# A decoder layer on one core: earlier ScalarE tables, query roots by logarithm and exponential, and a shorter TensorE program ahead of the head-pair loop

## The chip, the cores and the metric

The kernel runs on one core of one Trainium2 chip, in one launch. The metric is device time in microseconds. Three runs of the kernel before gave a median of 1426.36 us. All times below are microseconds from the start of the profiled span, unless ns is written.

## The reference

One decoder layer over x of 1024 tokens by 1024 channels, with 256 memory tokens. All of it is float32.

```
hn = rms_norm(x, attn_norm)
q, k, v, xq = split(hn @ sb_w_in, [1024, 1024, 1024, 256])
# stick-breaking attention, 16 heads of 64, causal
z = q k^T / 8
a = sigmoid(z) * product of sigmoid(-z) over the later keys before the query
mix = a v
# cross attention, 4 heads of 64, into the memory
mk, mv = split(rms_norm(mem, mem_norm) @ w_mem_kv, [256, 256])
p = softmax(rms_norm(xq per head, xq_norm) (rms_norm(mk per head, xk_norm))^T / 8)
cross = p mv
x = x + concat(mix, cross) @ w_out
x = x + (silu(h @ w_gate) * (h @ w_up)) @ w_down,   h = rms_norm(x, ffn_norm)
```

rms_norm(y, g) is y / sqrt(mean(y*y) + 1e-6) * g.

## The kernel before, in words

Every engine has its own program, with the order of its work written out by hand; semaphores join them. Operands of the large products are split in a high and a low part (names ending in _h and _l), and each product is three matmuls: high by high, high by low, low by high. ScalarE writes the high part (a Copy with rounding), VectorE the low part (a subtraction).

**Start.** SyncE loads x in 8 tiles of 128 tokens. For each tile `act_root` takes the sum of squares (Square with an accumulated sum) and the root of the mean (Sqrt), and `dve_scale` inverts the root and scales the tile. TensorE first runs WARM matmuls of the identity by the identity (128 columns, float32, result unused), then transposes x (L716). The first transposes wait until tiles 0 to 3 are scaled. The identity is made by GpSimd, which then fills `fail` with ones (L1561); `s_id` counts these constants.

**Memory and queries of the cross attention.** The queries of its four heads come in two groups of two heads, called `x_` 0 and 1. Those of group 1 are projected in the four pieces `pe_project_in(pe, MW, 0..3)` (L284, 12 matmuls of 512 columns each). The sum of squares of each query head is a matmul of the squared queries by `half_ones` (two columns): `pe_cross_stat(pe, x_)`, eight matmuls L843 in a row, for group 0 after piece 0 and for group 1 in turn 0 of the cross loop. Each float32 matmul stands in the records as two matmuls and two weight loads. `act_cross_stat` takes the root with Sqrt, `dve_cross_stat` inverts it and makes the scales `q_stat` for the softmax.

**Cross loop.** Sixteen turns c, written out without a loop instruction. In each, TensorE makes the scores of turn c+2 (L877), transposes the weights of turn c (L915), in every second turn sums the values (L944), and runs up to 12 matmuls L284 that project q, k and v for head pair 0 (`pe_piece`). ScalarE copies the transposed weights (`act_cross_high`) and takes Exp for turn c+2 (L897). The value sums and the sums of squares of both groups share one PSUM bank, `o_ps`. Then the first head pair is opened: scores L341, Sigmoid on ScalarE (L422, L428).

**Pair loop.** `pe_step` handles one head pair and projects the next pair's q, k, v (L313); it transposes the weights (L351), sums values (L367), and closes with the eight transposes of v (L324). Six of the steps are in a loop instruction with two steps in its body, run three times (376 matmuls a step). The output projection and the FFN follow; the FFN too has a loop instruction, run four times.

Of the kernel before, what the change touches and what calls it, by code (L numbers as in the profile page):

```python
# [19 lines left out]
def trunk(nc, x, mem, norms, w_mem_kv, w_out, w_gate, w_up, w_down, sb_w_in, out):  # L20
# [35 lines left out]
    with ExitStack() as ctx:  # L56
# [212 lines left out]
        def pe_project_in(pe, n, piece, out=j_ps, only=None, left=None):  # L269

            wh, wl = w_h[n // 2 % 2], w_l[n // 2 % 2]
            hf, q = (piece % 4) // 2, piece % 2
            if q == 0 and only != 1:
                pe.wait_ge(s_wl, n + hf + 1)
            for c in (2 * q, 2 * q + 1) if only is None else (2 * q + only,):
                kc = 4 * hf + c
                parts = [(i, half) for i in range(3) for half in range(2)]
                if kc == 0:
                    parts.sort(key=lambda p: p[1])
                for i, half in parts:  # L280
                    if kc == 0 and i == 0 and left:
                        left(half)
                    w, h = ((wh, hh), (wh, hl), (wl, hh))[i]
                    mm = pe.matmul(out[:, half], w[:, hf, c], h[:, kc, half * BANK:(half + 1) * BANK],  # L284
                                   start=(kc == 0 and i == 0), stop=(kc == KC - 1 and i == 2))
            if q == 1 and only != 0:
                mm.then_inc(s_pj, 1)

        def pe_piece(pe, s, piece, first=False, only=None):
            b = piece // 4  # L290

            def left(half):
                if first and b == 0:
                    pe.wait_ge(s_sq, 1 + half)
                else:
                    pe.wait_ge(s_eh, 6 * s + 2 * b - 1 + half)
                    if b:
                        pe.wait_ge(s_el, 4 * s + 2 * b - 1 + half)
            pe_project_in(pe, W0 + 6 * s + 2 * b, piece, only=only, left=left)
# [304 lines left out]
        s_ql = sem("cross_q_low_done")  # L604
        s_ct = sem("cross_weights_transposed")
# [73 lines left out]
        WARM = 12  # L679
# [156 lines left out]
        def pe_cross_stat(pe, x_):  # L836

            pe.wait_ge(s_sq, 2 * x_ + 2)
            if x_:
                pe.wait_ge(s_qr, 1)  # L840
            for c in range(x_ * NT, x_ * NT + NT):
                t = c % NT
                mm = pe.matmul(o_ps[:, 2 * c:2 * c + 2], xq_sq[:, x_, t * P:(t + 1) * P], half_ones[:, :],  # L843
                               start=True, stop=True)
            mm.then_inc(s_qs, 1)

        def act_cross_stat(act, x_):
            n = slice(2 * NT * x_, 2 * NT * (x_ + 1))
            act.wait_ge(s_qs, x_ + 1)
            act.activation(q_stat[:, 0, n], o_ps[:, n], ACT.Sqrt, bias=eps_col[:, :], scale=1.0 / HD).then_inc(s_qr, 1)  # L850

        def dve_cross_stat(dve, x_):
            n = slice(2 * NT * x_, 2 * NT * (x_ + 1))
            dve.wait_ge(s_qr, x_ + 1)
            dve.reciprocal(q_stat[:, 1, n], q_stat[:, 0, n]).then_inc(s_qi, 1)
            dve.wait_ge(s_qi, 3 * x_ + 1)
            dve.tensor_scalar(q_stat[:, 2, n], q_stat[:, 1, n], CQ, None, ALU.mult).then_inc(s_qi, 1)
            dve.tensor_scalar(q_stat[:, 3, n], q_stat[:, 1, n], -CQ, None, ALU.mult).then_inc(s_qi, 1)
            dve.wait_ge(s_qi, 3 * x_ + 3)
# [50 lines left out]
        def pe_cross_turn(pe, c):  # L910
            pe.wait_ge(s_cp, 2 * c + 2)
            if c >= 2:
                pe.wait_ge(s_ctl, c - 1)
            for b in range(4):
                mm = pe.transpose(t_ps[:, c % 2, b * P:(b + 1) * P], csucc[:, c % GR, b * P:(b + 1) * P], ident[:, :])  # L915
            mm.then_inc(s_ct, 1)
# [685 lines left out]
        def _(act):  # L1602
            act.wait_ge(s_id, 1)
            for t in range(4):
# [38 lines left out]
            for c in range(CU):  # L1643
                act_cross_high(act, c)
                if c == 0:
                    act_cross_stat(act, 1)
                if c + 2 < CU:
                    act_cross_exp(act, c + 2)
                if c in X_EVAC:
# [5 lines left out]
                if c in X_CONV:  # L1655
                    act_w(act, X_CONV[c] // 6, X_CONV[c] % 6, X_CONV[c] // 6)
            act.wait_ge(s_pj, W0 + 6)
# [59 lines left out]
        def _(dve):  # L1717
# [48 lines left out]
            for c in range(CU):  # L1766
# [8 lines left out]
                if c == 0:  # L1775
# [72 lines left out]
        def _(pe):  # L1848
            pe.wait_ge(s_id, 3)

            for _ in range(WARM):
                pe.matmul(ps[:, 3, 0:P], ident[:, :], ident[:, :], start=True, stop=True)
# [21 lines left out]
            pe_project_in(pe, MW, 0, xq_ps[1])  # L1874
            pe.wait_ge(s_id, MADE)
            pe.wait_ge(s_mka, MT + 2)
            pe.wait_ge(s_mv, MT)
            pe_cross_stat(pe, 0)
# [7 lines left out]
            pe_project_in(pe, MW, 2, xq_ps[1])  # L1886
            pe.wait_ge(s_xl, XU0)
# [5 lines left out]
            for c in range(CU):  # L1893
                if c + 2 < CU:
                    pe_cross_scores(pe, c + 2)
                if c == 0:
                    pe_cross_stat(pe, 1)
# [3 lines left out]
                for k in range(X_FIRST + sum(X_COUNT[:c]), X_FIRST + sum(X_COUNT[:c + 1])):  # L1901
                    pe_piece(pe, 0, k // 2, first=True, only=k % 2)
            pe_scores(pe, 0, 0, 0, first=True)
# [47 lines left out]
```

## Time and profile before

| what | value |
|---|---|
| median of 3 runs | 1426.36 us (1424.12 to 1427.22) |
| the profiled execution | 1431.33 us |
| its span | 1429.5 us |
| PE busy in the span | 96% |
| ACT busy, DVE busy | 46%, 66% |
| mean granted clock of PE | 0.981 |
| chain of work that ended last, by engine | PE 90%, ACT 4%, DVE 2%, issue 2% |

The profiled execution took 1.83 us beyond its span, and 4.97 us more than the median of the runs. PE is TensorE's matmuls, PEld its weight loads, ACT ScalarE, DVE VectorE, POOL GpSimd, SPq the queue of SyncE that issues transfers. A time in square brackets at the end of a line of the timeline is the idle time of the engine before it, with what ended it.

### The profile page before, as it was taken

To read this page: it belongs to the slowest core of one execution; us is meant where nothing else is said; L and a number is where in the kernel's file an instruction comes from. 1 tells how busy PE (TensorE), PEld (TensorE's weight loads), DVE (VectorE), ACT (ScalarE), POOL (GpSimd) and SP (SyncE) were. 2 spreads that over 40 slices of the span, in tenths; PEclk is the share of its full clock that TensorE was granted. 3 is DMA by queue.
4 is the path that set the end of the run, shared out by engine and by line. 5 is a ranking of instruction groups with operands and counts; after the bars stand their busy time and mean duration, and the time that the engine had idled before them with its cause. 6 is when DMAs were issued, how large, how long until landed. Compare 5 with 4: busy or idle time off the path is not lost.

```text
span 1429.5 us, 20494 instructions
## 1 busy us (share of the span) xinstructions
PE 1377.2 (96%) x6988; PEld 1127.6 (79%) x6988; DVE 949.7 (66%) x1346; ACT 655.3 (46%) x1120; POOL 186.3 (13%) x155
## 2 busy tenths in 40 slices
PE   6999999899989999699999999999999999999999
PEld 5777788788878888577887788888888888888887
DVE  5567879687968888786347857455565645656455
ACT  7566566566666666573245413324232232422321
POOL 0000000000000000214014311112111120211200
PEclk9989999999999999899999999999999999999999
DMA  6100101001000101003300212111112111121103
GB/s 236 30 17 22 30 23 31 24 23 30 23 23 23 37 17 44 30 23 110 104 16 15 89 52 66 45 47 43 63 42 64 51 44 59 44 60 58 44 30 133
DMA packets 90136, 70.23 MB, mean 49 GB/s; under 512 B 3792, under 2 KB 75472, under 8 KB 90064
## 3 DMA queue, kind: packets, MB, share of 16 engines
q1 hardware_dynamic: 90064, 69.23, 15.6%
q8 instruction: 50, 0.82, 0.3%
q14 instruction: 22, 0.18, 0.0%
HBM read 65.03 MB, written 4.19 MB: 48 GB/s over the span
## 4 chain that ended last, share of the span: by engine, by line
PE 90%; ACT 4%; DVE 2%; issue 2%; POOL 1%; DMA 1%; SPq 0%; ACTq 0%; DVEq 0%; POOLq 0%
PE ps L1284 27%; PE ps L313 17%; PE ps L1380 17%; PE ps L987 7%; PE ps L367 5%; PE ps L351 5%; PE ps L341 4%; PE ps L284 3%; PE ps L1064 1%; ACT junk L687 1%; PE ps L776 1%; POOL f L1144 1%; PE ps L716 1%; PE ps L915 1%; PE ps L877 1%
## 5 line engine op out<-in xcount | busy, mean ns | idle before, releaser
L1390 DVE TENSOR_TENSOR x<-ps,x 128x512 f32<-128x512 f32 x176 | 121.6, 691 | 71.2 <-PE ps L1380 67.0
L436 ACT ACTIVATE a_h<-ps 128x256 fp32r<-128x256 f32 (+2 forms) x96 | 78.0, 812 | 145.6 <-PE ps L351 145.6
L1296 ACT ACTIVATE kept<-ps 128x512 f32<-128x512 f32 x60 | 35.7, 595 | 236.0 <-PE ps L1284 236.0
L313 PE MATMUL ps<-hh,w_h 128*128 128x512 f32 x336 | 142.0, 423 | 0.0
L1380 PE MATMUL ps<-dw_h,gu_l 128*128 128x512 f32 x352 | 138.5, 394 | 0.0
L1380 PE MATMUL ps<-dw_l,gu_h 128*128 128x512 f32 x352 | 137.5, 391 | 0.0
L1380 PE MATMUL ps<-dw_h,gu_h 128*128 128x512 f32 x352 | 137.0, 389 | 0.3 <-issue 0.3
L313 PE MATMUL ps<-hh,w_l 128*128 128x512 f32 x336 | 133.5, 397 | 0.0
L313 PE MATMUL ps<-hl,w_h 128*128 128x512 f32 x336 | 133.1, 396 | 0.0
L545 DVE TENSOR_TENSOR a_l<-ps,a_h 128x256 fp32r<-128x256 f32 (+2 forms) x96 | 91.5, 953 | 60.5 <-ACT a_h L436 59.9
L1284 PE MATMUL ps<-ft_h,part_l 128*128 128x512 f32 x320 | 126.5, 395 | 0.0
L1284 PE MATMUL ps<-ft_l,part_h 128*128 128x512 f32 x320 | 125.2, 391 | 0.0
L1284 PE MATMUL ps<-ft_h,part_h 128*128 128x512 f32 x320 | 124.5, 389 | 0.0
L519 DVE TENSOR_TENSOR_SCAN fail<-fail,own 128x129 f32<-128x129 f32 (+3 forms) x128 | 107.7, 869 | 1.3 <-ACT fail L422 1.3
L1254 DVE TENSOR_TENSOR part_l<-part_x,part_h 128x512 fp32r<-128x512 f32 x140 | 94.3, 691 | 5.3 <-ACT part_h L1247 2.8
L351 PE MATMUL ps<-ident,succ 128*128 128x128 f32 x576 | 82.0, 279 | 13.6 <-DVE a_l L545 8.6
L1284 PE MATMUL ps<-f_h,part_l 128*128 128x512 f32 x240 | 94.7, 395 | 0.0
L1284 PE MATMUL ps<-f_h,part_h 128*128 128x512 f32 x240 | 93.5, 389 | 0.6 <-DVE part_l L1254 0.6
L1284 PE MATMUL ps<-f_l,part_h 128*128 128x512 f32 x240 | 93.8, 391 | 0.0
L532 DVE TENSOR_TENSOR succ<-fail,succ 128x256 f32<-128x256 f32 (+2 forms) x96 | 93.6, 975 | 0.3
L1308 DVE TENSOR_TENSOR kept<-ps,kept 128x512 f32<-128x512 f32 x30 | 20.7, 691 | 104.0 <-PE ps L1284 104.0
L552 POOL TENSOR_TENSOR o_t<-o_t,pv_low 128x256 f32 x24 | 23.7, 986 | 497.8 <-ACT o_t L448 497.8
(217 smaller groups left out, 3141.9 us busy)
## 6 DMA issues: line engine op xcount, KB each, us to landing
w_raw<-in_sb_w_in SPq DMA_DIRECT2D x52, 256.0 KB, 2.9
dw_x<-in_w_down SPq DMA_DIRECT2D x22, 512.0 KB, 3.3
part_x<-in_w_gate SPq DMA_DIRECT2D x40, 256.0 KB, 3.5
part_x<-in_w_up SPq DMA_DIRECT2D x40, 256.0 KB, 2.9
wo_raw<-in_w_out SPq DMA_DIRECT2D x20, 256.0 KB, 2.8
x_in<-in_x SPq DMA_DIRECT2D x8, 512.0 KB, 7.8
x<-in_x SPq DMA_DIRECT2D x16, 256.0 KB, 5.7
out<-x SPq DMA_DIRECT2D x16, 256.0 KB, 2.0
```

Source lines behind the costliest of these rows:

```text
L313: mm = pe.matmul(j_ps[:, 0], w[:, kc // 4, kc % 4], h[:, kc, half * BANK:(half + 1) * BANK], start=(kc == 0 and i == 0), stop=(kc == KC - ...
L351: mm = pe.transpose(t_ps[:, h, j * P:(j + 1) * P], succ[:, u % 2, h, j * P:(j + 1) * P], ident[:, :])
L367: mm = pe.matmul(o_ps[:, h * 2 * P + q0:(h + 1) * 2 * P], v_s[par][:, k0 // P + j, 2 * h:2 * h + 2, :].rearrange("p a d -> p (a d)"), a[:, ...
L436: act.activation(a_h[:, :, 0:w // P, col * P:(col + 1) * P], t_ps[:, :, 0:w].rearrange("p h (j q) -> p h j q", q=P), ACT.Copy).then_inc(s_ ...
L519: dve.tensor_tensor_scan(back, back, own[:, BANK - w:BANK + 1][:, ::-1], 0.0, ALU.mult, ALU.max).then_inc(s_scan, 1)
L532: done = dve.tensor_tensor(g, f[:, :, 1:w + 1], g, ALU.mult)
L545: dve.tensor_tensor(a_l[:, :, 0:w // P, c], t_ps[:, :, 0:w].rearrange("p h (j q) -> p h j q", q=P), a_h[:, :, 0:w // P, c].bitcast(F32), A ...
L987: mm = pe.matmul(out_bank(i), o[k][:, t * P:(t + 1) * P], w[:, k], start=(at_ == 0 and j == 0), stop=(at_ == len(order) - 1 and j == 2))
L1254: dve.tensor_tensor(part_l[m][p][:, :, :].rearrange(flat), part_x[m][p][:, :, :].rearrange(flat), part_h[p][:, :, :].rearrange(flat).bitca ...
L1284: mm = pe.matmul(product_bank(m, p), w[:, k], g[:, k], start=(p in (0, 1, 3) and k == 0 and i == 0), stop=(k == 3 and i == 2), skip_group_ ...
L1380: mm = pe.matmul(ps[:, (2, 3, 0, 1)[d % 4]], g[:, fb, t * P:(t + 1) * P], w[n][:, fb], start=(fb == 0 and i == 0), stop=(fb == FB - 1 and ...
L1390: dve.tensor_tensor(o, ps[:, (2, 3, 0, 1)[d % 4]], o, ALU.add).then_inc(s_x2, 1)
```

## The change

- ScalarE gets two activations whose results nobody reads: a Sqrt of one column before it waits for the first tile of x, and a Sigmoid of one column in turn 13 of the cross loop.
- The root and its reciprocal for the queries are taken as exp(-0.5 ln(mean + eps)): Ln, then Exp on ScalarE, in place of Sqrt on ScalarE and a reciprocal on VectorE.
- The eight small matmuls of group 0 are placed one by one behind the first eight large matmuls of piece 0, and write to the bank of the scores, `z_ps[:, 1]`, in place of `o_ps`. Those of group 1 move from turn 0 to turn 1 of the cross loop, four behind each of its two half pieces. ScalarE's part for group 1 moves behind Exp of turn 3, VectorE's part to turn 2.
- The first matmuls are 5 of 512 columns (identity by `fail`, float32) in place of 12 of 128 columns, and wait for the fourth constant in place of the third.
- TensorE no longer waits for `s_ctl` before the transposes of turns 2 to 15.

```
-        def pe_project_in(pe, n, piece, out=j_ps, only=None, left=None):
+        def pe_project_in(pe, n, piece, out=j_ps, only=None, left=None, stat=None):
...
+                    if stat is not None and stat % NT < 6 * (c % 2) + 2 * i + half + 1 <= NT:
+                        pe_cross_stat(pe, stat // NT * NT + 6 * (c % 2) + 2 * i + half)
...
-        WARM = 12
+        WARM = 5
...
-        def pe_cross_stat(pe, x_):
-
-            pe.wait_ge(s_sq, 2 * x_ + 2)
-            if x_:
-                pe.wait_ge(s_qr, 1)
-            for c in range(x_ * NT, x_ * NT + NT):
-                t = c % NT
-                mm = pe.matmul(o_ps[:, 2 * c:2 * c + 2], xq_sq[:, x_, t * P:(t + 1) * P], half_ones[:, :],
-                               start=True, stop=True)
-            mm.then_inc(s_qs, 1)
+        def cross_stat_ps(x_):
+            return (z_ps[:, 1], o_ps)[x_]
+
+        def pe_cross_stat(pe, c):
+
+            x_, t = c // NT, c % NT
+            if t == 0:
+                pe.wait_ge(s_sq, 2 * x_ + 2)
+            mm = pe.matmul(cross_stat_ps(x_)[:, 2 * t:2 * t + 2], xq_sq[:, x_, t * P:(t + 1) * P], half_ones[:, :],
+                           start=True, stop=True)
+            if t == NT - 1:
+                mm.then_inc(s_qs, 1)
 
         def act_cross_stat(act, x_):
             n = slice(2 * NT * x_, 2 * NT * (x_ + 1))
             act.wait_ge(s_qs, x_ + 1)
-            act.activation(q_stat[:, 0, n], o_ps[:, n], ACT.Sqrt, bias=eps_col[:, :], scale=1.0 / HD).then_inc(s_qr, 1)
+            act.activation(q_stat[:, 0, n], cross_stat_ps(x_)[:, 0:2 * NT], ACT.Ln, bias=eps_col[:, :], scale=1.0 / HD
+                           ).then_inc(s_ql2, 1)
+            act.wait_ge(s_ql2, x_ + 1)
+            act.activation(q_stat[:, 1, n], q_stat[:, 0, n], ACT.Exp, scale=-0.5).then_inc(s_qr, 1)
 
         def dve_cross_stat(dve, x_):
             n = slice(2 * NT * x_, 2 * NT * (x_ + 1))
             dve.wait_ge(s_qr, x_ + 1)
-            dve.reciprocal(q_stat[:, 1, n], q_stat[:, 0, n]).then_inc(s_qi, 1)
-            dve.wait_ge(s_qi, 3 * x_ + 1)
...
         def pe_cross_turn(pe, c):
             pe.wait_ge(s_cp, 2 * c + 2)
-            if c >= 2:
-                pe.wait_ge(s_ctl, c - 1)
...
             act.wait_ge(s_id, 1)
+            act.activation(rms[:, 0:1], eps_col[:, :], ACT.Sqrt)
...
             for c in range(CU):
                 act_cross_high(act, c)
-                if c == 0:
-                    act_cross_stat(act, 1)
                 if c + 2 < CU:
                     act_cross_exp(act, c + 2)
+                if c == 1:
+                    act_cross_stat(act, 1)
...
+                if c == CU - 3:
+                    act.activation(x_stat[:, 0, 0:1], eps_col[:, :], ACT.Sigmoid)
...
-                if c == 0:
+                if c == 2:
                     dve_cross_stat(dve, 1)
...
-            pe.wait_ge(s_id, 3)
-
+            pe.wait_ge(s_id, 4)
             for _ in range(WARM):
-                pe.matmul(ps[:, 3, 0:P], ident[:, :], ident[:, :], start=True, stop=True)
+                pe.matmul(ps[:, 3], ident[:, :], fail[:, 0, 0, 0:BANK], start=True, stop=True)
...
-            pe_project_in(pe, MW, 0, xq_ps[1])
             pe.wait_ge(s_id, MADE)
-            pe.wait_ge(s_mka, MT + 2)
-            pe.wait_ge(s_mv, MT)
-            pe_cross_stat(pe, 0)
+            pe_project_in(pe, MW, 0, xq_ps[1], stat=0)
             pe_project_in(pe, MW, 1, xq_ps[1])
...
             pe_project_in(pe, MW, 2, xq_ps[1])
+            pe.wait_ge(s_mv, MT)
+            pe.wait_ge(s_qr, 1)
             pe.wait_ge(s_xl, XU0)
             pe_cross_scores(pe, 0)
...
                 if c == 0:
-                    pe_cross_stat(pe, 1)
+                    pe.wait_ge(s_sq, 2 * XP)
                 pe_cross_turn(pe, c)
                 if c % 2 == 0 and c:
                     pe_cross_values(pe, c // 2 - 1)
-                for k in range(X_FIRST + sum(X_COUNT[:c]), X_FIRST + sum(X_COUNT[:c + 1])):
+                k0 = X_FIRST + sum(X_COUNT[:c])
+                for k in range(k0, k0 + X_COUNT[c]):
                     pe_piece(pe, 0, k // 2, first=True, only=k % 2)
+                    if c == 1:
+                        for t in range(4 * (k - k0), 4 * (k - k0) + 4):
+                            pe_cross_stat(pe, NT + t)
```

## Rows read from the trace of the kernel before

**Rows 1.** The page: busy time, share of the span, instructions, by engine.

```profile
PE 1377.2 (96%) x6988; PEld 1127.6 (79%) x6988; DVE 949.7 (66%) x1346; ACT 655.3 (46%) x1120; POOL 186.3 (13%) x155
```

**Rows 2.** Windows: stretch, its length, busy time (instructions) by engine, granted clock.

```profile
57.60:61.00 3.40, 3.40 (x10) 2.60 (x9) 0.78 (x3) 0.03 (x1) 0.00 (x0) 0.50 0.27 77
74.60:84.90 10.30, 8.99 (x27) 6.59 (x26) 4.00 (x12) 6.96 (x14) 0.00 (x0) 0.50 0.09 27
142.90:146.40 3.50, 3.50 (x11) 2.58 (x9) 2.55 (x4) 0.00 (x0) 0.00 (x0) 0.51 0.00 0
264.00:391.50 127.50, 122.85 (x756) 101.86 (x755) 103.13 (x127) 81.10 (x131) 7.90 (x8) 0.99 0.09 26
854.30:975.50 121.20, 121.20 (x530) 99.13 (x529) 69.66 (x101) 35.85 (x61) 20.72 (x17) 1.00 0.18 53
```

**Rows 3.** Timeline of the start, all engines: start, length, instruction.

```profile
1.47 1.82 POOL L1561 MEMSET fail<- 128x2064 f32 x1
...
1.58 5.22 PE L1852 MATMUL ps<-ident 128*128 128x128 f32 x24 [1.58 <-POOL ident L1559]
...
4.20 1.28 ACT L687 ACT_TABLE_LOAD   x1 [4.20 <-DMA x_in<-in_x]
...
6.66 1.28 ACT L689 ACT_TABLE_LOAD   x1
...
10.89 1.04 ACT L687 ACTIVATE junk<-x_in 128x1024 f32<-128x1024 f32 x1
...
13.39 3.52 PE L716 MATMUL ps<-ident,x_in 128*128 128x128 f32 x16 [6.59 <-DVE x_in L696]
```

**Rows 4.** DMA issues of 2.62 to 2.65: size, us from issue to landing.

```profile
x_in<-in_x SPq DMA_DIRECT2D x1, 512.0 KB, 7.3
```

**Rows 5.** Timeline of the cross attention and the loop's opening, all engines.

```profile
54.88 1.92 PE L843 MATMUL ps<-half_ones,xq_sq 128*128 128x2 f32 x16 [0.26 <-DVE mv L1749]
...
61.09 0.60 PE L1883 MATMUL ps<-ident,mk_raw 128*128 128x128 f32 x4
...
71.47 0.38 PE L877 MATMUL ps<-mk_h,q_h 64*128 64x256 f32 x2
...
76.85 1.28 ACT L897 ACT_TABLE_LOAD   x1
...
78.85 0.58 PE L877 MATMUL ps<-mk_h,q_h 64*128 64x256 f32 x1 [1.31 <-ACT succ L897]
...
85.51 0.39 PE L877 MATMUL ps<-mk_h,q_h 64*128 64x256 f32 x2
...
...
86.47 0.36 PE L944 MATMUL ps<-a_h,mv 128*128 128x256 f32 x1
...
140.28 0.44 PE L341 MATMUL ps<-k_h,q_h 64*128 64x384 f32 x2 [1.41 <-ACT succ L428]
```

**Rows 6.** Timeline of PE in the pair loop: one place of each step, and the jumps.

```profile
210.38 0.66 PE L351 MATMUL ps<-ident,succ 128*128 128x128 f32 x4 [1.01 <-DVE a_l L545]
...
268.86 0.44 PE L341 MATMUL ps<-k_h,q_h 64*128 64x384 f32 x2 [2.62 <-issue]
276.10 0.66 PE L351 MATMUL ps<-ident,succ 128*128 128x128 f32 x4 [1.02 <-DVE a_l L545]
337.61 0.66 PE L351 MATMUL ps<-ident,succ 128*128 128x128 f32 x4 [1.01 <-DVE a_l L545]
...
396.74 0.69 PE L341 MATMUL ps<-k_h,q_h 64*128 64x384 f32 x2 [3.19 <-issue]
...
404.96 0.66 PE L351 MATMUL ps<-ident,succ 128*128 128x128 f32 x4 [1.02 <-DVE a_l L545]
```

**Rows 7.** Transfers of program code, 264.2 to 265.4: packets, MB.

```profile
q8 instruction: 2, 0.03, 17.7%
```

**Rows 8.** The same, 265.4 to 392.4.

```profile
q8 instruction: 7, 0.11, 0.4%
```

**Rows 9.** The same, 854 to 1339, the whole run of the FFN loop.

```profile
q8 instruction: 5, 0.08, 0.1%
```

More of the change, by code:

```diff
@@ L285, in pe_project_in, with pe_piece @@
                                    start=(kc == 0 and i == 0), stop=(kc == KC - 1 and i == 2))
+                    if stat is not None and stat % NT < 6 * (c % 2) + 2 * i + half + 1 <= NT:
+                        pe_cross_stat(pe, stat // NT * NT + 6 * (c % 2) + 2 * i + half)
             if q == 1 and only != 0:
                 mm.then_inc(s_pj, 1)
-        def pe_piece(pe, s, piece, first=False, only=None):
+        def pe_piece(pe, s, piece, first=False, only=None, stat=None):
             b = piece // 4
@@ L298, in left @@
                         pe.wait_ge(s_el, 4 * s + 2 * b - 1 + half)
-            pe_project_in(pe, W0 + 6 * s + 2 * b, piece, only=only, left=left)
+            pe_project_in(pe, W0 + 6 * s + 2 * b, piece, only=only, left=left, stat=stat)
         def pe_part(pe, s, par, p, lo):
@@ L604, in trunk @@
         s_ql = sem("cross_q_low_done")
+        s_ql2 = sem("cross_q_logs_taken")
         s_ct = sem("cross_weights_transposed")
@@ L854, in dve_cross_stat @@
             dve.wait_ge(s_qr, x_ + 1)
-            dve.reciprocal(q_stat[:, 1, n], q_stat[:, 0, n]).then_inc(s_qi, 1)
-            dve.wait_ge(s_qi, 3 * x_ + 1)
             dve.tensor_scalar(q_stat[:, 2, n], q_stat[:, 1, n], CQ, None, ALU.mult).then_inc(s_qi, 1)
             dve.tensor_scalar(q_stat[:, 3, n], q_stat[:, 1, n], -CQ, None, ALU.mult).then_inc(s_qi, 1)
-            dve.wait_ge(s_qi, 3 * x_ + 3)
+            dve.wait_ge(s_qi, 2 * x_ + 2)
         def dve_cross_q(dve, b):
```

## The prediction

> **What bounds the kernel.** I read the page first: TensorE is busy for 1377.2 us of the span of 1429.5 [rows 1], and it carries 90% of the chain of waits, so only what lets TensorE start earlier, wait less or run at a higher clock counts. Then the granted clock by windows, which shows stretches at half clock (1.2 GHz, the other level being 2.4). Three of them lie in the part that the change touches: 57.6 to 61.0, 74.6 to 84.9, 142.9 to 146.4 [rows 2]. A matmul of 512 columns costs 0.23 us at full clock (121.2 us for 530 [rows 2]), so a stretch at half clock loses half of the time that TensorE is busy in it. Last I read the timeline ahead of each stretch, to see what TensorE did before its clock fell, and the program code transfers around the jumps of the two loops.
>
> **1. The start: 1.1 us.** ScalarE loads a table when x arrives, at 4.20, and another for Sqrt at 6.66 [rows 3]. The new Sqrt moves one load ahead of the wait and makes the other needless: Square runs under Sqrt's table too (10.89, no load before it [rows 3]). That is twice 1.28 us off ScalarE, but x doesn't come so early. Tile 3 is issued at 2.62 and takes 7.3 us [rows 4]: it lands at 9.95 or so, and its Square can begin at 10.05 in place of 10.89. So 0.84 us, and the first transposes start at 12.55 in place of 13.39. They ran before at half clock (16 in 3.52 us against 0.60 us for 4 at 61.09 [rows 3, 5]). TensorE had ended its first matmuls at 6.8, and waited 6.59 us. The new ones have 4 times the columns for 5/12 of the count: 1.67 x 5.22 = 8.7 us at the rate of [rows 3], less if the clock rises on the way, from 3.3 (the fill of `fail` ends then [rows 3]). They end between 9 and 12.0, before 12.55. If the clock then stands at full, the first copy by ScalarE starts 0.3 to 0.6 us earlier. I take 0.84 + 0.3 = 1.1, bounds 0.5 and 1.5. From there the same chain of roots leads on, and tile 4 (behind the four) isn't late by more than it was.
>
> **2. Sums of squares, group 0: 1.7 us.** From 54.88 to 61.09 TensorE does 16 small matmuls in 1.8 us and 12 large ones. At full clock that is 1.8 + 12 x 0.23 = 4.6 us; it took 6.2, and 0.26 of idle stood before it [rows 5]. The clock fell right behind the small ones. Spread between large matmuls, no stretch holds small ones alone for more than 0.25 us, so I take it that the clock stays: 1.6 + 0.26, less 0.2 for weight loads that the mixing bares. Bounds: 0.1 if the clock falls all the same, 1.9. ScalarE's Ln and Exp, with loads, lie in its wait for the transposes at 61.09.
>
> **3. Group 1: 3.9 us.** From 71.47 to 85.51 TensorE spends 14.0 us [rows 5]. What is in it at full clock: two sets of scores and two of transposes (0.96 us a turn, from 85.51 to 86.47 [rows 5]) 1.9, small matmuls 1.8, 18 large ones 4.2; sum 7.9. The other 6.1 are half clock over 9.0 busy us [rows 2] and the wait of 1.31 for Exp, which stood behind Sqrt and two loads (the second at 76.85 [rows 5]). The price of the new order: the value sums of turn 2 share a bank with the small sums, and wait until ScalarE's Exp for group 1 is done. The traces place a load by the next function alone: a set without Sqrt at 4.20, then another [rows 3]. So I expect Ln to load a set of its own, and Exp to load the old one again: 2 x 1.28 + 2 x 0.3 = 3.2 us from the last small matmul, of which TensorE covers 0.96 with scores and transposes. It waits 2.2 us; queued behind are six large matmuls and the scores of turn 5, and ScalarE's Exp for turn 4 waits too, which nobody needs before those. 6.1 - 2.2 = 3.9. Bounds: 2.2 (the clock falls in that wait, 1.7 us as at 57.6) and 6.1 (no load between Ln and Exp, no wait).
>
> The Trainium skill ("ScalarE: Activation LUTs", Table sets: the hidden batching unit) says that ln and then exp cost one load, since one set holds both. No row here shows Ln. By that rule, if the set is the one chosen, a load is spared and the wait of this step shrinks to about 0.9 us or nothing: 5.2 to 6.1 in place of 3.9.
>
> **4. The loop's opening: 2.8 us.** The load for Sigmoid stood between the last copies of the cross loop and the first Sigmoid; TensorE waited 1.41 us for it at 140.28 [rows 5]. In turn 13 ScalarE has waits that hold a load. That gives 1.3. With 1.3 of 2.5 us idle gone, the half clock from 142.9 to 146.4 [rows 2] likely goes too: 1.7 us more. I take 1.3 + 1.5; bounds 1.3 and 3.0. If the cover were gone, the load would delay the copies of turn 14 by 1.28 us.
>
> **5. The jumps of the pair loop: 9.9 us.** A step takes 61.51 us (276.10 to 337.61), but 65.72 (210.38 to 276.10) and 67.35 (337.61 to 404.96) where the loop jumps back [rows 6]: 4.2 and 5.8 dearer, made of idle 2.62 and 3.19 with nobody to wait for, and of a lower clock behind it. Program code comes in pieces of 16 KB. At the jump two are fetched within 1.2 us [rows 7], 7 more in the rest of the pass [rows 8], the last of them (392.4) just ahead of the next jump. So from one jump to the next there are 9 pieces, the first being the loop's head, which is fetched again each time: it had been dropped. The FFN loop is jumped three times with no fetch at all: 5 pieces in its first pass, none later [rows 9]. Its body has 530 matmuls against 752 [rows 2], or 6 pieces touched and one fetched ahead: 7 are kept, 9 aren't. The last piece of the pair loop is entered just before the jump: 1.1 us lies at most between the two fetches of [rows 7], in which TensorE does 8 or 9 matmuls with their loads, some 20 instructions. The change takes away 7 float32 matmuls of two matmuls and two loads, and 14 waits: 42 instructions ahead of the loop. The loop then ends in the piece before, and its passes need 8. If 8 are kept, both jumps cost nothing: 10.0 less 0.1. Below, nothing is saved if they aren't.
>
> The Trainium skill ("Runtime: NRT & Kernel Launch", Instruction fetch mechanics) gives TensorE room for 2048 instructions in blocks of 16 KiB; an estimate from it is 8 blocks, so the loop would just fit. The same section says that a jump outside a window of two pages forces a fetch. By that the jumps go on costing 10.0 us whatever the place; [rows 9] speak against it, a loop of more than four pieces without a fetch.
>
> The dropped waits for `s_ctl` are met anyway: VectorE does the low part of turn c-2 ahead of the weights of turn c. The missing reciprocal and the moved VectorE part lie in its idle time. Nothing.
>
> **Sum.** 1.1 + 1.7 + 3.9 + 2.8 + 9.9 = 19.4 us. The profiled execution took 1431.33 (span 1429.5 and 1.83 around it): 1411.9. The median of the runs lies 4.97 lower; I carry that over: 1407.0.
>
> **Rivals.**
> - *The head of the pair loop is still fetched at each jump* (8 pieces aren't kept, or the distance is over 42 instructions). For it: no row shows 8 kept. Against it: 7 are. Steps 1 to 4 alone: 9.5 us, 1416.9. Chance 0.22.
> - *The clock falls in spite of the spreading,* in steps 2, 3 and 4, the loop fits: 1.6 + 1.7 + 1.5 = 4.8 us back, 1411.8. For it: the new wait of 2.2 us. Against: a wait of 1.41 and more were needed at 140. Chance 0.12.
> - *Ln and Exp share one load:* 1405. Chance 0.15.
> - *Slower: the FFN loop loses its head.* If only 7 pieces are kept and the shift made that loop touch one more, its three jumps would each cost 4.2 to 5.8 us, 12.6 to 17.5 in all, and the pair loop would save nothing: 9.5 - 15 gives 1432. It decides from the point where the loop's end crosses into another piece or its head falls back into one. The last fetch comes 9.5 us ahead of the first jump at 975.5, some 41 matmuls, so 42 instructions don't take it over. Chance 0.02.
>
> **How the numbers follow.** The forecast, all five steps with a load for Ln and one for Exp, has 0.49: 1407.0, on its own 1403 to 1412. The first rival reaches to 1421, with its likely part up to 1418.5. Range 1402.5 to 1418.5, some 0.15 outside. A change of 0.2% (2.9 us) is about what a measurement tells from none. Faster by more: 0.95; within: 0.03; slower: 0.02.
>
> **What would show it.** No table load after 4.20 until the queries' Ln; first transposes near 12.5; full clock from 57 to 85; a wait of the value sums of turn 2 for Exp (2 us, or none with one load); no load in front of the first Sigmoid and no idle of 1.4 us there; six steps of 61.5 us, and no program code fetched in the second and third pass of the pair loop. The forecast is wrong above all if the steps with a jump keep their 65 to 67 us.

## The result, and the profile after

The changed kernel takes 1409.97 us (median of 4 runs, 1409.1 to 1410.26); the kernel before took 1426.79 beside it (4 runs, 1424.12 to 1429.02). The ratio is 0.9882, 95% interval 0.9866 to 0.9898: faster by 1.2%, and inside the forecast's range of 1402.5 to 1418.5, 3 us above its centre of 1407.0. The profiled execution took 1409.1 (span 1407.3), 22.2 us less than that of before.

The page: TensorE's busy time fell by 12.2 us, with 14 matmul records less. Beside [rows 1]:

```profile
PE 1365.0 (97%) x6974; PEld 1115.6 (79%) x6974; DVE 948.7 (67%) x1344; ACT 655.8 (47%) x1124; POOL 186.6 (13%) x155
```

The windows, with the granted clock as the first figure behind the busy times. In answer to [rows 2], the stretches around the old 57.6, 74.6 and 142.9, and the pair loop's passes: the clock is 1.00 in all of them, which is the 2.4 GHz level. Behind the pair loop half clock remains (0.90 from 512 to 600, and a short stretch near 744).

```profile
52.00:58.00 6.00, 6.00 (x33) 5.05 (x33) 3.50 (x15) 3.88 (x6) 0.00 (x0) 1.00 0.00 0
66.00:86.00 20.00, 19.06 (x123) 15.12 (x122) 13.80 (x41) 14.39 (x35) 0.00 (x0) 1.00 0.09 27
126.00:146.00 20.00, 17.75 (x114) 13.95 (x113) 15.17 (x22) 13.79 (x27) 0.40 (x1) 1.00 0.06 16
150.00:512.00 362.00, 355.91 (x2216) 295.84 (x2214) 302.28 (x371) 237.50 (x379) 22.38 (x23) 1.00 0.09 25
```

The timeline of the start, which answers [rows 3]. One table load, at 0.75, while x is on its way; the first matmuls are 6.50 us long; the transposes start 0.87 us earlier and take 1.97 us in place of 3.52.

```profile
0.75 1.28 ACT L1608 ACT_TABLE_LOAD   x1 [0.75 <-PEq L1948]
2.04 0.20 ACT L1608 ACTIVATE rms<-eps_col 128x1 f32<-128x1 f32 x1
3.34 6.50 PE L1858 MATMUL ps<-fail,ident 128*128 128x512 f32 x10 [3.34 <-POOL fail L1565]
12.52 1.97 PE L719 MATMUL ps<-ident,x_in 128*128 128x128 f32 x16 [2.68 <-DVE x_in L699]
```

The timeline of the cross attention and the opening, in answer to [rows 5]. Ln (L855) and Exp (L858) have a table load each, in both groups. The second Ln's load is at 74.29, but its Ln only at 76.23, behind the last small matmul: the load stands ahead of the wait. The value sums of turn 2 (L948) wait 0.85 us for Exp. Sigmoid's load, at 121.51, lies in the cross loop, and the opening's waits at L343 are 0.56 and 0.68. Before they were 1.41 and 1.11; the last line is the second of these, from the kernel before.

```profile
52.74 1.28 ACT L855 ACT_TABLE_LOAD   x1
54.04 0.27 ACT L855 ACTIVATE q_stat<-ps,eps_col 128x16 f32<-128x16 f32 x1
54.33 1.28 ACT L858 ACT_TABLE_LOAD   x1
...
57.46 0.60 PE L1886 MATMUL ps<-ident,mk_raw 128*128 128x128 f32 x4
...
74.29 1.28 ACT L855 ACT_TABLE_LOAD   x1
76.23 0.27 ACT L855 ACTIVATE q_stat<-ps,eps_col 128x16 f32<-128x16 f32 x1 [0.66 <-PE ps L847]
76.53 1.28 ACT L858 ACT_TABLE_LOAD   x1
77.82 0.21 ACT L858 ACTIVATE q_stat<-q_stat 128x16 f32<-128x16 f32 x1
...
78.18 0.36 PE L948 MATMUL ps<-a_h,mv 128*128 128x256 f32 x1 [0.85 <-ACT q_stat L858]
...
121.51 1.28 ACT L1663 ACT_TABLE_LOAD   x1
...
131.12 0.44 PE L343 MATMUL ps<-k_h,q_h 64*128 64x384 f32 x2 [0.56 <-DVE o_t L966]
...
132.59 0.50 PE L343 MATMUL ps<-k_h,q_h 64*128 64x512 f32 x2 [0.68 <-ACT succ L430]
```

```profile
142.17 0.50 PE L341 MATMUL ps<-k_h,q_h 64*128 64x512 f32 x2 [1.11 <-ACT succ L428]
```

TensorE's timeline in the pair loop: one and the same place of its first three steps (L353 is the L351 of [rows 6]), called the mark of a step from here on, and the first scores behind the two jumps. The marks of the next three steps are at 322.44, 384.01 and 445.55, and that of the step behind the loop is at 507.10. From mark to mark it is 61.5 to 61.6 us whether there is a jump between them or not, and no idle time stands in front of the scores at 255.12 and 378.28, where [rows 6] had 2.62 and 3.19.

```profile
137.79 0.66 PE L353 MATMUL ps<-ident,succ 128*128 128x128 f32 x4 [1.01 <-DVE a_l L547]
...
199.33 0.66 PE L353 MATMUL ps<-ident,succ 128*128 128x128 f32 x4 [1.01 <-DVE a_l L547]
...
255.12 0.44 PE L343 MATMUL ps<-k_h,q_h 64*128 64x384 f32 x2
...
260.85 0.66 PE L353 MATMUL ps<-ident,succ 128*128 128x128 f32 x4 [1.02 <-DVE a_l L547]
...
378.28 0.44 PE L343 MATMUL ps<-k_h,q_h 64*128 64x384 f32 x2
```

The DMA queues from 243.5 to 500, the second and third pass (the loop ends near 500): data only. The kernel before fetched 9 pieces of program code in each of these passes (from 264.8 to 392.6 and from there to 521).

```profile
q1 hardware_dynamic: 13200, 6.56, 8.9%
```

Over the whole span the kernel before fetched 50 pieces and the changed one 32, which is these 18 less (from the two pages):

```profile
q8 instruction: 50, 0.82, 0.3%
q8 instruction: 32, 0.52, 0.2%
```

**Where the 22.2 us come from**, by the starts of the same instruction in the two profiled executions:

| up to | before | after | gained so far | in this stretch | forecast |
|---|---|---|---|---|---|
| first large matmul of the first piece of q | 51.66 | 50.09 | 1.57 | 1.57 | 1.1 |
| mk transposes | 61.09 | 57.46 | 3.63 | 2.06 | 1.7 |
| value sums of turn 2 | 86.47 | 78.18 | 8.29 | 4.66 | 3.9 |
| mark of the pair loop's first step | 148.87 | 137.79 | 11.08 | 2.79 | 2.8 |
| mark of the step behind the loop | 528.09 | 507.10 | 20.99 | 9.91 | 9.9 |
| end of the span | 1429.5 | 1407.3 | 22.2 | 1.2 | 0 |

These are differences of one execution against one. The runs below show how far the old program's own stretches vary: from the mk transposes to the value sums of turn 2 it took 25.38 us here, 24.61 in e3, 25.39 in e3c, 24.21 in e2 and 22.63 in e3b (in e3b with the very same instructions, in the others with one wait less). The changed kernel took 20.72.

### The profile page after: what moved, and what is told of

Same layout as the page of the kernel before. It is cut to its first block and busy times, and to the rows that moved or that the text cites. A ratio compares the mean times of both kernels' runs of the same rounds, so it can differ in the third digit from the quotient of the medians.

```text
span 1407.3 us, 20453 instructions
## 1 busy us (share of the span) xinstructions
PE 1365.0 (97%) x6974; PEld 1115.6 (79%) x6974; DVE 948.7 (67%) x1344; ACT 655.8 (47%) x1124; POOL 186.6 (13%) x155
## 5 line engine op out<-in xcount | busy, mean ns | idle before, releaser
L353 PE MATMUL ps<-ident,succ 128*128 128x128 f32 x576 | 81.4, 278 | 13.5 <-DVE a_l L547 8.6
```

The lines of the kernel that those rows point to most:

```text
L353: mm = pe.transpose(t_ps[:, h, j * P:(j + 1) * P], succ[:, u % 2, h, j * P:(j + 1) * P], ident[:, :])
```

## The experiments

The kernels that ran together shared their runs of the kernel before. Its median was 1426.53 for e1 to e3b (23 runs), 1426.94 for e4 to e7 (7) and 1427.61 for e8, e9, e10 and e3c (9).

### e1: the changed kernel, longer again ahead of the pair loop

```diff
             for _ in range(WARM):
                 pe.matmul(ps[:, 3], ident[:, :], fail[:, 0, 0, 0:BANK], start=True, stop=True)
+            for _ in range(11):
+                pe.matmul(ps[:, 3, 0:2], ident[:, :], ident[:, 0:2], start=True, stop=True)
```

> The changed kernel with 11 more float32 matmuls of 2 columns behind its first five; that puts 44 instructions ahead of the pair loop again, two more than the change took away. Theory (the loop's head is dropped from the kept code when the loop's end lies in one more piece): program code is fetched in the second and third pass again, the two steps with a jump take 65 to 67.5 us in place of 61.6, and the time is 9 to 10 us above the changed kernel, 1418 to 1420. Rival (the steps became shorter for another reason, such as where in its phases the loop is entered): all steps stay at 61.5 us, 1409 to 1411.

Measured: 1416.25 us (1415.59 to 1419.11, 5 runs), ratio to before 0.9925 (0.9912 to 0.9938). That is 6.3 over the changed kernel; the two intervals don't overlap. Its timeline shows the step with the first jump, 67.0 us from mark to mark, and the idle time ahead of the first scores behind it (the second jump's is 2.58, at 386.54):

```profile
199.53 0.66 PE L353 MATMUL ps<-ident,succ 128*128 128x128 f32 x4 [1.01 <-DVE a_l L547]
257.91 0.69 PE L343 MATMUL ps<-k_h,q_h 64*128 64x384 f32 x2 [2.50 <-issue]
266.53 0.66 PE L353 MATMUL ps<-ident,succ 128*128 128x128 f32 x4 [1.02 <-DVE a_l L547]
```

Its queue of program code from 240 to 510 (one piece at the end of the first pass, at 253.4, and 9 in each of the next two):

```profile
q8 instruction: 19, 0.31, 0.5%
```

From the first mark (137.96) to the fifth (393.78) it needs 9.6 us more than the changed kernel (137.79 to 384.01). The added 44 instructions stand in the wait for the first x, and its first mark is only 0.17 us later; so it is the place of the loop in the program, and nothing in the loop, that makes its jumps dear. In the profile the price came out as expected; in the median it is smaller, 6.3 and not 9 to 10.

### e2: the kernel before with only the shortening

```diff
-        WARM = 12
+        WARM = 5
...
             pe.wait_ge(s_cp, 2 * c + 2)
-            if c >= 2:
-                pe.wait_ge(s_ctl, c - 1)
```

The first matmuls stay at 128 columns. 42 TensorE instructions are gone, and nothing else of the change is in it. The dots stand for lines left out.

> The kernel before with only its TensorE program made 42 instructions shorter: 5 first matmuls in place of 12, and the waits for s_ctl left out. Theory: six equal steps of 61.5 us, no code fetched in passes two and three, 8 to 10 us faster than before, 1417 to 1419. Rival (the gain of the pair loop isn't from the length of the code): the steps with a jump stay at 65 to 67 us and the time at 1426 to 1428, or more, since the shorter first matmuls only lose clock.

Measured: 1418.3 us (1416.08 to 1421.63, 6 runs), ratio 0.9942 (0.9929 to 0.9956), 8.2 below the kernel before. Marks of its first, third and fifth step: 123.1 and 123.0 us for two steps, with a jump in each pair.

```profile
146.13 0.66 PE L351 MATMUL ps<-ident,succ 128*128 128x128 f32 x4 [1.01 <-DVE a_l L545]
...
269.23 0.66 PE L351 MATMUL ps<-ident,succ 128*128 128x128 f32 x4 [1.02 <-DVE a_l L545]
...
392.26 0.66 PE L351 MATMUL ps<-ident,succ 128*128 128x128 f32 x4 [1.02 <-DVE a_l L545]
```

With e1 this shows it from both sides: the shortening alone frees the jumps, and without it none of the rest does. It gives about half of the whole gain: 8.2 us in medians, and e2 is 8.3 above the changed kernel, which is what the other four steps give together. In its profile e2 also comes to the first mark 2.74 us before the kernel before. That is clock ahead of the loop (none of it half at 57, and 3.4 us of half clock in place of 10.2 in group 1); e3b, with the same instructions up to 57, is at half clock there, so it varies from execution to execution.

### e3, e3b, e3c: where the border lies

Three kernels as e2, but with fewer instructions taken away. e3: WARM = 12, the 14 waits gone (14 less). e3b: WARM = 5, the waits kept (28 less). e3c: WARM = 7, the waits gone (34 less). They have 10, 10 and 5 runs.

> The kernel before with 14 instructions less (only the waits for s_ctl left out). Theory: the piece border is some 18 to 20 instructions ahead of the jump, so 14 aren't enough: jumps stay dear, 1425 to 1428. Rival (the waits themselves cost): 1 us or more faster.

> The kernel before with 28 instructions less (only 5 first matmuls in place of 12). Theory: past the border, so both jumps are free, 1417 to 1419. If the border lay more than 28 instructions ahead of the jump, the time would stay at 1426 to 1428.

> The kernel before with 34 TensorE instructions less ahead of the pair loop (5 of its first matmuls of four instructions, and the 14 waits for s_ctl). With 28 less the two jumps were dear, with 42 less they were not. It narrows the place of the border: if the head of the loop is kept, all steps take 61.5 us and the time is 6 to 10 us below the kernel before, 1417 to 1421; if not, two steps take 65 to 67 us and the time is that of the kernel before. I give both the same chance. A time between (one jump dear) would speak against a border at all.

| instructions less | median | ratio, interval | idle at the two jumps | pieces fetched in the span |
|---|---|---|---|---|
| 14 | 1427.2 | 1.0000 (0.9988 to 1.0012) | 3.07, 3.39 | 50 |
| 28 | 1426.7 | 0.9999 (0.9983 to 1.0014) | 2.75, 2.62 | 50 |
| 34 | 1418.4 | 0.9938 (0.9924 to 0.9953) | none | 32 |
| 42 (e2) | 1418.3 | 0.9942 (0.9929 to 0.9956) | none | 32 |

The rows behind the table's second line: e3b's first scores behind both jumps.

```profile
267.53 0.45 PE L341 MATMUL ps<-k_h,q_h 64*128 64x384 f32 x2 [2.75 <-issue]
...
394.82 0.69 PE L341 MATMUL ps<-k_h,q_h 64*128 64x384 f32 x2 [2.62 <-issue]
```

e3c's marks of the first, third and fifth step are at 148.86, 271.98 and 394.98, 123.1 and 123.0 us apart.

It is a step and not a slope: six instructions decide over some 8 us, the rest over nothing. The border lies between 28 and 34 instructions, which misses my "some 20", and e3b's expectation with it: I gave 28 the better chance. The change's 42 had 8 to 14 to spare. e3c starts its loop where the kernel before does (148.86 against 148.87), so its 9.2 us are the jumps' own, as far as a median tells. Its 34 are 20 of matmuls and their loads and 14 waits. Since 28 of the first kind alone were too few, the waits count in the distance too.

### e4: Sqrt and reciprocal in the new places

```diff
-            act.activation(q_stat[:, 0, n], ..., ACT.Ln, bias=eps_col[:, :], scale=1.0 / HD).then_inc(s_ql2, 1)
-            act.wait_ge(s_ql2, x_ + 1)
-            act.activation(q_stat[:, 1, n], q_stat[:, 0, n], ACT.Exp, scale=-0.5).then_inc(s_qr, 1)
+            act.activation(q_stat[:, 0, n], ..., ACT.Sqrt, bias=eps_col[:, :], scale=1.0 / HD).then_inc(s_qr, 1)
...
+            dve.reciprocal(q_stat[:, 1, n], q_stat[:, 0, n]).then_inc(s_ql2, 1)
+            dve.wait_ge(s_ql2, x_ + 1)
```

> The changed kernel with Sqrt and VectorE's reciprocal again, in the new places. Theory (Ln and Exp bring nothing by themselves, since each has its own table load): group 0 needs no load for Sqrt, group 1 the same two loads. The value sums of turn 2 then wait for Sqrt alone, and not for the second load and Exp behind it, so TensorE's wait of 0.85 us there goes: 0.5 to 1 us faster than the changed kernel, 1409 to 1409.5. Rival (ln and exp are what shortens group 1): 2 us or more slower than the changed kernel, 1412 or above.

Measured: 1409.06 us (1408.67 to 1409.65, 4 runs), ratio 0.9874 (0.9857 to 0.9890). ScalarE's loads in this part are three in place of four (Sqrt in group 0 needs none; the first is at 59.74), and the two of group 1:

```profile
74.66 1.28 ACT L855 ACT_TABLE_LOAD   x1
...
78.32 1.28 ACT L903 ACT_TABLE_LOAD   x1
```

The value sums of turn 2 start at 77.43 without a wait; the load at 78.32 comes back as a wait of 0.45 us of scores at 85.06. At the mark of the first step e4 is 0.49 us behind the changed kernel, of which 0.37 come from a later x. So ln and exp, as made here, bring nothing over Sqrt in the same places. The sign of the difference is as expected, its size (0.9 us in the median) is inside the spread of the runs.

### e5 and e6: the small matmuls in a row again

e5, group 0:

```diff
-            pe_project_in(pe, MW, 0, xq_ps[1], stat=0)
+            pe_project_in(pe, MW, 0, xq_ps[1])
+            for t in range(NT):
+                pe_cross_stat(pe, t)
```

e6, group 1, all eight ahead of turn 1's transposes in place of four behind each of two half pieces:

```diff
                     pe_cross_scores(pe, c + 2)
+                if c == 1:
+                    for t in range(NT):
+                        pe_cross_stat(pe, NT + t)
...
-                    if c == 1:
-                        for t in range(4 * (k - k0), 4 * (k - k0) + 4):
-                            pe_cross_stat(pe, NT + t)
```

> The changed kernel with group 0's eight small matmuls in a row behind piece 0. Theory (small matmuls in a row let the clock fall): half clock for 3.4 us behind them, near 55 to 58, and the transposes L1886 at 59 to 59.3 in place of 57.46: 1.5 to 1.8 us slower, 1411 to 1412. Rival (it was the wait for VectorE ahead of them, or chance, and not the row): full clock, at most 0.3 us slower.

> The changed kernel with group 1's eight small matmuls in a row, ahead of the transposes of turn 1. Theory: half clock behind them for 3.4 us or more, between 72 and 80, 1.5 to 3 us slower, 1411 to 1413; the wait of the value sums gets shorter, since Ln comes 3 us earlier. Rival (the long half clock of before came from the wait for Exp, not from the row): full clock, and up to 0.8 us faster.

Measured: e5 1409.27 us (1408.89 to 1410.49), ratio 0.9873 (0.9857 to 0.9890); e6 1409.92 (1408.63 to 1411.22), ratio 0.9876 (0.9859 to 0.9892), 4 runs each. e5's timeline has the small matmuls in one row, and its window has the clock at 1.00 all the same; the mk transposes are at 57.56, 0.10 later than in the changed kernel, as its first transposes are (12.62).

```profile
52.98 1.84 PE L847 MATMUL ps<-half_ones,xq_sq 128*128 128x2 f32 x16
...
57.56 0.60 PE L1888 MATMUL ps<-ident,mk_raw 128*128 128x128 f32 x4
```

```profile
48.00:58.00 10.00, 10.00 (x56) 8.46 (x54) 4.49 (x16) 5.09 (x10) 0.00 (x0) 1.00 0.15 46
```

e6's profile does show a half-clock stretch of 3.4 us behind its row. ScalarE's Exp no longer makes anybody wait there. From the mk transposes to the value sums it takes 21.29 us, 0.57 more than the changed kernel, and its median is that of the changed kernel. It was also slow at the start, where its program is the changed kernel's: x came 0.44 us later, TensorE had stood still for 3.60 us in place of 2.68, and the 16 transposes took 3.54 us at half clock (from 13.15 to 16.56).

```profile
74.80:78.20 3.40, 3.40 (x10) 2.69 (x9) 0.71 (x2) 3.35 (x8) 0.00 (x0) 0.53 0.23 64
```

So in group 0 the theory that the row alone makes the clock fall is refuted, and in group 1 it is possible, not shown by one execution, and worth nothing that a median shows.

### e7 and e9: the two halves of the start

e7 takes the early Sqrt away (`act.activation(rms[:, 0:1], eps_col[:, :], ACT.Sqrt)`), and nothing else. e9 leaves the first matmuls short:

```diff
-            pe.wait_ge(s_id, 4)
+            pe.wait_ge(s_id, 3)
             for _ in range(WARM):
-                pe.matmul(ps[:, 3], ident[:, :], fail[:, 0, 0, 0:BANK], start=True, stop=True)
+                pe.matmul(ps[:, 3, 0:P], ident[:, :], ident[:, :], start=True, stop=True)
```

> The changed kernel without the first Sqrt. Theory: two table loads on ScalarE again, tile 3's Square at 10.89, first transposes at 13.39 in place of 12.52, 0.9 us slower, and up to 0.7 more if the clock falls in the longer wait: 1411 to 1411.6. Rival (the transfers bound the start so that the load is hidden altogether): no difference.

> The changed kernel with its five first matmuls cut to 128 columns of the identity, which no longer wait for the fill of the fail buffer. They then end near 3 us in place of 9.84, and TensorE idles for some 9 us ahead of the first transposes. Theory: the first transposes run at half clock again (3.5 us for 16 in place of 1.97), the start of the chain of roots is 0.3 to 0.6 us later, and what follows the transposes hides part of it: 0.3 to 1.5 us more, 1410.3 to 1411.5. Rival: ScalarE's roots set the chain and the transposes are not on it: within 0.2 us of 1410.0.

Measured: e7 1410.21 us (1409.56 to 1410.56), ratio 0.9880 (0.9864 to 0.9897); e9 1410.01 (1409.17 to 1411.79), ratio 0.9881 (0.9864 to 0.9897), 4 runs each. Both do at the start what was expected. e7's two loads are back (4.29 and 6.75), and its transposes are 0.97 us later than in the changed kernel:

```profile
4.29 1.28 ACT L690 ACT_TABLE_LOAD   x1 [4.29 <-DMA x_in<-in_x]
13.49 0.77 PE L719 MATMUL ps<-ident,x_in 128*128 128x128 f32 x5 [2.52 <-DVE x_in L699]
```

e9's transposes start in time and take 3.67 us, as long as at half clock. (The granted clock from 12 to 17 is given as 1.00 all the same, so here I go by the durations.)

```profile
12.51 3.67 PE L719 MATMUL ps<-ident,x_in 128*128 128x128 f32 x16 [8.43 <-DVE x_in L699]
```

In e7's profile the 1.0 us is still there at 57 and at the end (span 1408.3). In e9's, 0.73 us is there at 57, 0.65 at the mark behind the pair loop and 0.1 at the end; the stretch behind the loop varies by more than that between executions of one and the same code (below). Neither shows in a median: 0.2 and 0.0 us over the changed kernel, under the expectations of 1.0 to 1.6 and 0.3 to 1.5.

### e8: without the early Sigmoid

```diff
-                if c == CU - 3:
-                    act.activation(x_stat[:, 0, 0:1], eps_col[:, :], ACT.Sigmoid)
```

> The changed kernel without the early Sigmoid in turn 13, so that the load of Sigmoid's table stands again between the last copies of the cross loop and the first Sigmoid of the pair loop. Theory (step 4 of the prediction): TensorE waits 1.3 us more at the loop's first scores, and if that brings the stretch at half clock back, another 1.5 to 1.7: the mark of the first pass (L349 to L353, at 137.79 in the changed kernel) comes 1.3 to 3.0 us later, and the time is 1411.3 to 1413.0. Rival: the 2.78 us that the changed kernel gained there come from the other edits (the clock stays up because of what is ahead), and the load alone is hidden: under 0.5 us, 1410.0 to 1410.5.

Measured: 1412.81 us (1411.46 to 1413.39, 4 runs), ratio 0.9893 (0.9877 to 0.9909), 2.8 over the changed kernel. The load stands in front of the first Sigmoid, and the scores of the opening wait 1.42 and 1.10 us:

```profile
130.29 1.28 ACT L424 ACT_TABLE_LOAD   x1
...
132.29 0.44 PE L343 MATMUL ps<-k_h,q_h 64*128 64x384 f32 x2 [1.42 <-ACT succ L430]
...
134.19 0.50 PE L343 MATMUL ps<-k_h,q_h 64*128 64x512 f32 x2 [1.10 <-ACT succ L430]
```

and right behind them the clock is 0.53 for 3.5 us:

```profile
135.50:139.00 3.50, 3.50 (x10) 2.76 (x9) 2.01 (x3) 0.00 (x0) 0.00 (x0) 0.53 0.03 8
```

The mark of the first step is at 140.92, 3.13 later, of which 0.3 comes from a later x. The two waits are 1.28 us longer than the changed kernel's 0.56 and 0.68, the length of the load; the other 1.5 of the 2.8 come with the half clock behind them. The rival (hidden) is out.

### e10: one table set for both functions, loaded by hand

One line ahead of the root of group 0:

```diff
+            act.preload_act_table_set("natural_log_exp_and_others")
```

> The changed kernel with one table set that holds both ln and exp loaded by hand ahead of the root of group 0. Theory (one load serves Ln, Exp and the exponentials of the cross attention): the loads at 54.33, 74.29 and 76.53 are gone, the wait of 0.85 us of the value sums of turn 2 is gone, and the time is 0.5 to 0.9 us shorter, 1409.1 to 1409.5, as with Sqrt in the same places (1409.06). Rival: a load is placed in front of each function all the same, and the time is that of the changed kernel or, with one load more, up to 1.3 us longer (1410.0 to 1411.3).

Measured: 1407.69 us (1407.53 to 1410.23, 4 runs, three of them at 1407.5 to 1407.7), ratio 0.9866 (0.9849 to 0.9883). ScalarE's timeline: one load, then Ln and Exp of both groups and all of the cross attention's exponentials without another, up to Sigmoid's.

```profile
52.89 1.28 ACT L1639 ACT_TABLE_LOAD   x1
54.19 0.27 ACT L855 ACTIVATE q_stat<-ps,eps_col 128x16 f32<-128x16 f32 x1
54.49 0.22 ACT L858 ACTIVATE q_stat<-q_stat 128x16 f32<-128x16 f32 x1
...
76.67 0.21 ACT L858 ACTIVATE q_stat<-q_stat 128x16 f32<-128x16 f32 x1
```

The value sums of turn 2 follow at 77.22, with nothing in front of them, where the changed kernel has 78.18:

```profile
77.22 0.36 PE L948 MATMUL ps<-a_h,mv 128*128 128x256 f32 x1
```

That is the best of the versions that ran: 2.3 us under the changed kernel's median. The intervals of the two ratios overlap (0.9849 to 0.9883, 0.9866 to 0.9898), and one of its four runs is at the changed kernel's time; the trace accounts for the 0.96 us at 78.18 (1.1 less 0.16 for a later x), and not for the rest. At the mark of the first step it is 0.99 us ahead of the changed kernel.

## Why the prediction was right, and where it was off

**1. The start (1.1 forecast).** 1.57 us in the profile by the first large matmul of q, just over the upper bound of 1.5. The 0.84 at the first transposes was 0.87, the first matmuls ended at 9.84 in the 9 to 12 forecast, and the transposes ran at full clock. What was too small was the share of the transposes' clock: I took 0.3, it was 0.7, and e9's 0.73 is the same number. It isn't had in every execution: e6, with the same start, lost the clock there. In medians this step can't be seen (e7, e9).

**2. Group 0 (1.7).** 2.06 us, again just over the upper bound (1.9). The stretch at half clock is gone and so is the wait of 0.26. The reason given was wrong: I put the fall of the clock down to 16 small matmuls in a row, and e5 has the row and loses neither clock nor time. The 0.2 us taken off for weight loads that the mixing bares isn't there either: from the first large matmul of q to the mk transposes it is 7.37 us with the small matmuls spread and 7.39 with them in a row (e5). Nor does the code alone decide the clock: e2 and e3b have the same TensorE instructions up to there, and in their profiles e3b is at half clock from 56.8 to 60.2 and e2 is not. Half clock stood there in four of the five profiles with the old order (all but e2) and in none of the nine with the new start of group 0, e5 with its row among them. What does decide it, and whether taking away the wait ahead of the row helps, stays open.

**3. Group 1 (3.9).** 4.66 us, in the bounds, but against an execution of the kernel before at the dear end of its own spread: against e3b, which had no half clock there, it would be 1.91, below the lower bound of 2.2. The step to name is the wait of 2.2 us: it was 0.85. Ln and Exp did each get a load, as taken from the traces, but Ln's load was issued ahead of Ln's own wait (74.29), so only Exp's 1.28 lay behind the last small matmul. The 6.1 that the rest should have given was 5.5; in the prediction half of 9.0 busy us and the wait of 1.31 add up to 5.8 and not 6.1. The Trainium skill ("ScalarE: Activation LUTs", Table sets: the hidden batching unit) has ln followed by exp at one load, since one set holds both: the changed kernel's trace shows two (52.74, 54.33), e10's shows one. The set that serves both exists; it isn't the one that was chosen for Ln.

**4. The opening (2.8).** 2.79 us, from both parts, the load and the clock behind it. e8 gives it back in the profile (2.8 net of the later x) and in the median (2.8). All six profiles with the load in the old place (e8 and the five of the old order) have half clock right behind the opening, and the eight with it in the new place don't.

**5. The jumps (9.9).** 9.91 us in the profile, and no code fetched in the second and third pass. e1 and e2 show it from both sides. Wrong in it is the distance to the border, "some 20 instructions": over 28 and at most 34. I had counted the matmuls that TensorE does in the 1.1 us between the last fetch of a pass and that of the head. That time says nothing of the distance: at the second jump of the same kernel it is 0.2 us (392.5 and 392.7), and in e3b, whose loop ends 28 instructions nearer to the border, it is 0.5 and 1.6. The forecast held because 42 was over both, and that was luck, since no row gave the distance. The count of pieces fits every run. The four kernels with dear jumps (before, e1, e3, e3b) fetch 7 pieces in the loop's first pass, 9 in each later one, and 50 in all; the ten others fetch 6, none, and 32. One piece less in the first pass makes 8 needed in place of 9. That 8 is what can be kept, and not something else that changes when the loop's end crosses a border, is the simplest reading and wasn't tested in another way. Eight is also the estimate from the Trainium skill ("Runtime: NRT & Kernel Launch", Instruction fetch mechanics), and the trace agrees, with no fetch from 243.5 to 500. That section's other rule, a forced fetch at a jump outside two pages, isn't borne out here: the changed kernel fetched 6 pieces in its loop's first pass (141.0 to 242.9), and the jump back over them fetched nothing.

**The sum and the median.** The profile gained 22.2 us against a sum of 19.4. The steps above account for 1.6 of the difference; 1.2 more arose behind the pair loop, where the change has no instruction. From the loop's end to the first jump of the FFN loop, 14 profiled executions took 452.9 to 455.3 us, with or without a short half-clock stretch near 745 to 768; before was at 455.0 and after at 453.8. So 1.2 us is within what varies from execution to execution, and no effect of the change is seen there.

The step that put the forecast 3 us low is the last one, "I carry that over": it took 4.97 us off for the difference between the profiled execution and the median. It amounts to taking gains read in one execution for gains in the median. The profiled execution of before was a dear one, and the changed kernel's was not (1409.1, median 1409.97). In all three stretches that vary, it stands at or near the dear end: 25.38 us in group 1, where the old program took 22.63 to 25.39; 10.0 us for its two jumps, where the four kernels with dear jumps paid 8.6 to 10.0; 455.0 behind the loop, out of 452.9 to 455.3. In medians the change gave 16.8 us and not 19.4: 8.2 from the jumps (e2; 9.2 in e3c, 6.3 in e1), forecast 9.9, and 8.3 from the other steps, forecast 9.5. So the sum was 2.8 too small for the profiles and 2.6 too large for the medians, and that the forecast lay only 3 us off is partly luck: the sum was short by 2.8 and the step to the median took off 5.8 too much, which cancel in part.

All four kernels with dear jumps were profiled above their medians (by 4.5, 2.9, 1.3 and 0.7 us), the ten others between 1.3 below and 2.2 above. Whether dear jumps make the runs spread isn't shown: theirs spread over 3.5 to 10.2 us and those of the others over 1.0 to 2.7, but with 5 to 23 runs against mostly 4, e2 without them spread over 5.5, and the kernel before itself, with them, over 2.9 in its 7 runs beside e4 to e7.

**The rivals.** The head still fetched (1416.9): out, by the marks; e1 shows what it would have given, 1416.25. The clock falling in spite of the spreading: out, 1.00 throughout. One load for Ln and Exp (1405): not in the changed kernel, and in e10 it gave 1 us by the trace and 2.3 by the median, where I had put 2. The FFN loop losing its head: no sign of it; from its first jump to the end it is 453.9 us in both profiles.

## What to carry to other kernels

When a loop's first instructions after a jump show idle time with no releaser, look at the program code transfers: if each pass fetches the loop's head again, count how many pieces the loop touches; here 34 instructions less ahead of it were worth 8 to 9 us, and 28 less were worth nothing. Look at where each table load lands in the trace, since two functions that could share a set may get two, and a load that TensorE has to wait for can cost as much again by the clock behind the wait. And before a forecast in medians is summed from one profiled execution that lies well above its median, look at a second execution of the same kernel: a stretch that was dear only once is no gain for the median.

## What the runs showed of the hardware that was not expected

- A table load can be done ahead of the wait of the activation that needs it: loaded at 74.29, Ln at 76.23, with 0.66 us of waiting between them.
- Waits of 1.42 and 1.10 us in front of TensorE, in place of 0.56 and 0.68, cost 2.8 us and not 1.28: behind them stood 3.5 us at a clock of 0.53 (e8).
- Sixteen matmuls of two columns in a row, 1.84 us, left the clock at 1.00 (e5) in the place where it had fallen before.
- The same instructions had no half clock in one execution and 10.2 us of it in another (group 1, e3b and the kernel before), which made 2.75 us.
- A loop that had fetched 6 pieces of code in its first pass jumped back over them with no fetch; one that had fetched 7 fetched 9 in every later pass.
